# YOCO step on one Trainium2 core: layer 0's sample states decayed by ScalarE a stage earlier, value rows spread from two row groups, and layer 1's attention turn split off

## The reference, cut to what matters

```python
def gla_recurrent(q, k, v, g, s0):
    def step(s, xs):
        qt, kt, vt, gt = xs
        s = jnp.exp(gt)[..., None] * s + kt[..., None] * vt[..., None, :]
        return s, jnp.einsum('bhk,bhkv->bhv', qt, s)
```

```python
        p1 = jax.nn.softmax(jnp.einsum('bqhd,bkhd->bhqk', qf[..., :DH_B], k1) + bias, axis=-1)
        p2 = jax.nn.softmax(jnp.einsum('bqhd,bkhd->bhqk', qf[..., DH_B:], k2) + bias, axis=-1)
        return jnp.einsum('bhqk,bkhv->bqhv', p1 - lam * p2, vf)
```

## Time and profile before

| | before |
|---|---|
| median of 3 runs | 2008.17 us |
| profiled execution, whole | 2010.52 us |
| its span | 2008.7 us |
| TensorE matmul busy | 78% |
| VectorE busy | 38% |
| ScalarE busy | 19% |
| GpSimd busy | 17% |
| DMA, mean over the span | 280 GB/s |
| mean granted TensorE clock | 0.876 |

### The profile page before, as it was taken

How to read it: one execution, slowest core, us unless ns; L and a number is a source line. 1 busy time by engine, 2 the same in 40 slices (tenths; PEclk the granted TensorE clock), 3 DMA queues, 4 the chain that set the end, 5 groups by cost and what they waited for, 6 DMA issues and landing times. The chain is left out here.

```text
span 2008.7 us, 22067 instructions
## 1 busy us (share of the span) xinstructions
PE 1573.5 (78%) x7466; PEld 723.7 (36%) x7467; DVE 762.4 (38%) x1300; ACT 390.5 (19%) x755; POOL 341.1 (17%) x266
## 2 busy tenths in 40 slices
PE   6999976767479998936899887777587499989960
PEld 3333335233233333303356553344343233333320
DVE  1010125486300000136855567996385300000008
ACT  1010022022021221222120002334222012222212
POOL 0000000000000000022745566550000000000004
PEclk8989997589599999967999988889888699999985
DMA  8652620531699899979969999884422599999962
GB/s 329 254 218 84 253 85 1 186 135 53 262 406 427 337 383 430 390 285 347 355 241 393 402 375 404 338 321 164 145 92 94 217 372 377 422 428 427 429 258 93
DMA packets 122908, 563.02 MB, mean 280 GB/s; under 512 B 13621, under 2 KB 43126, under 8 KB 101307
## 3 DMA queue, kind: packets, MB, share of 16 engines
q1 hardware_dynamic: 98450, 496.63, 62.4%
q10 hardware_dynamic: 15424, 33.08, 4.3%
q0 software_dynamic: 8944, 32.15, 4.3%
HBM read 521.80 MB, written 40.03 MB: 280 GB/s over the span
## 5 line engine op out<-in xcount | busy, mean ns | idle before, releaser
L1483 PE MATMUL ps<-arena_w,arena_r 128*64 128x512 f32 x1664 | 379.2, 612 | 33.7 <-issue 28.8
L1483 PEld LDWEIGHTS ps<-arena_w,arena_r 128*64 128x64 f32 x1664 | 126.3, 142 | 280.4 <-issue 274.1
L1465 PE MATMUL ps<-arena_w,arena_r 128*64 128x512 f32 x832 | 190.1, 605 | 19.3 <-ACT arena_r L1513 19.3
L1560 DVE TENSOR_TENSOR arena_r<-arena_r,ps 128x512 f32<-128x512 f32 x38 | 26.1, 688 | 442.7 <-ACT arena_r L1530 442.7
L1863 POOL TENSOR_TENSOR arena_w<-arena_w,arena_r 128x1024 f32<-128x1024 f32 x48 | 114.9, 2400 | 110.3 <-DMA arena_w<-in_cache_k_dram 109.9
L1916 PE MATMUL ps<-arena_w,xt 128*128 128x256 f32 x512 | 123.8, 404 | 1.4 <-ACT xt L2081 1.4
L1863 POOL TENSOR_TENSOR arena_r<-arena_r 128x1024 f32<-128x1024 f32 x48 | 116.0, 2419 | 52.4 <-DMA arena_r<-in_cache_k_dram 52.1
L447 PE MATMUL ps<-arena_w,xt 128*128 128x512 f32 x256 | 112.5, 596 | 0.4 <-PE ps L206 0.4
L999 PE MATMUL ps<-arena_w,xt 128*128 128x512 f32 x256 | 111.4, 593 | 0.0
L1916 PEld LDWEIGHTS ps<-arena_w,xt 128*128 128x128 f32 x512 | 102.7, 203 | 17.9 <-ACT xt L2081 1.5
L1465 PEld LDWEIGHTS ps<-arena_w,arena_r 128*64 128x64 f32 x832 | 57.4, 139 | 125.7 <-issue 103.9
(11 more groups left out here) (367 smaller groups left out, 1978.8 us busy)
## 6 DMA issues: line engine op xcount, KB each, us to landing
arena_w<-in_w_exp_gate_dram SPq DMA_DIRECT2D x38, 2048.0 KB, 15.4
arena_w<-in_w_exp_up_dram SPq DMA_DIRECT2D x38, 2048.0 KB, 16.6
arena_w<-in_w_exp_down_dram SPq DMA_DIRECT2D x38, 2048.0 KB, 17.0
arena_m<-in_cache_v_dram SPq DMA_DIRECT2D x128, 512.0 KB, 7.9
arena_w<-in_cache_k_dram SPq DMA_DIRECT2D x64, 512.0 KB, 8.6
arena_r<-in_cache_k_dram SPq DMA_DIRECT2D x64, 512.0 KB, 9.8
arena_w<-in_w_ada_dram SPq DMA_DIRECT2D x12, 2048.0 KB, 16.8
arena_m<-in_w_ada_dram SPq DMA_DIRECT2D x12, 2048.0 KB, 8.7
```

The lines of the kernel that those rows point to most:

```text
L1465: last = nc.tensor.matmul(psy[c][at:at + 64, :], ht[u][:, k, 64 * (1 - a):64 * (2 - a)], wd[u][:, k, c * 512:(c + 1) * 512], start=(k == 0 ...
L1483: last = nc.tensor.matmul(ps[at:at + 64, :], xgt[u][:, k, 64 * a:64 * (a + 1)], w[u][:, k, :], start=(k == 0), stop=(k == KT - 1), tile_po ...
L1560: V.tensor_tensor(hs[u], es[u], psu[:, :], ALU.mult).then_inc(h_ok, 1)
```

## The change

Layer 0: the states are loaded into `arena_m`, at the head of SyncE's queue in the prompt's stage and ahead of the fill of `y_rows` (whose source becomes `m.x`). ScalarE decays them there, 32 activations between its own steps, and the sample stage starts at the products. The upper half of each value row is written a second time, to partitions 32 to 39; there are two selectors, at partitions 0 and 32, and the two spreading products sit in different row groups of the array. Layer 1: `turn(u - 2)` (the turning part of `finish`) is issued ahead of `scores(u)`; `keep` moves from VectorE to ScalarE; the two maxima become one instruction; ScalarE's `c_copy` comes ahead of `second_weight`; ScalarE issues the loads of the own value weights, after the wait it had anyway; the load at L1824 comes one step later.

```diff
@@ stage_gla_project, ScalarE
+                if c == 1:
+                    nc.scalar.copy(m.v[32:32 + NS, NTT - 1, 512:1024], m.ps[1][0:NS, :])
@@ stage_gla_prompt
+    m.st, src = view(m.M, 0, NS * HA, DVA), a["state_gla"].rearrange("l b h k v -> k (l b h) v")
+            def decay(b0, b1):
+                for b in range(b0, b1):
+                    s.wait_ge(st_in[b // 2], 16)
+                    for h in range(HA):
+                        nc.scalar.activation(m.st[:, b * HA + h, :], m.st[:, b * HA + h, :], ACT.Copy, scale=eg[:, h, b:b + 1])
+            nc.scalar.activation(eg, m.gs, ACT.Exp).then_inc(eg_ok, 1)
...
             exponents(2)
+            s.wait_ge(eg_ok, 1)
+            decay(0, 2)
             key_rows(2)
             output(1)
             exponents(3)
+            decay(2, 4)
             key_rows(3)
+            decay(4, 6)
             output(2)
+            decay(6, 8)
             output(3)
@@ stage_gla_prompt, SyncE
+            for n in range(NS // 2):
+                c = slice(2 * n * HA, 2 * (n + 1) * HA)
+                sp.dma_start(m.st[:, c, :], src[:, c, :]).then_inc(st_in[n], 16)
@@ stage_gla_sample, GpSimd
-            nc.gpsimd.memset(sel, 0.0).then_inc(sel_ok, 1)
+            for n in range(2):
+                nc.gpsimd.memset(sel[n], 0.0).then_inc(sel_ok, 1)
+            for n in range(2):
+                g.wait_ge(sel_ok, n + 1)
+                blocks = sel[n].rearrange("r (b n) -> r b n", n=P)
+                nc.gpsimd.affine_select(out=blocks, in_=blocks, compare_op=ALU.not_equal, fill=1.0, base=0,
+                                        pattern=[[-1, NS], [0, P]], channel_multiplier=1).then_inc(dg_ok, 1)
@@ stage_gla_sample, VectorE
-                v.wait_ge(st_in[b // 2], 16)
-                for h in range(HA):
-                    nc.vector.tensor_scalar(st[:, b * HA + h, :], st[:, b * HA + h, :], eg[:, h, b:b + 1], None, ALU.mult)
-                v.wait_ge(vb_mm, b + 1)
-                v.drain()
+                v.wait_ge(vb_mm, 2 * b + 2)
@@ stage_gla_sample, TensorE
-                    last = nc.tensor.matmul(m.ps[2 * (b % 2) + n][:, :], sel[:, b * P:(b + 1) * P],
-                                            m.v[0:NS, NTT - 1, n * 512:(n + 1) * 512], start=True, stop=True)
-                last.then_inc(vb_mm, 1)
+                    nc.tensor.matmul(m.ps[2 * (b % 2) + n][:, :], sel[n][:, b * P:(b + 1) * P],
+                                     m.v[32 * n:32 * n + NS, NTT - 1, n * 512:(n + 1) * 512], start=True, stop=True,
+                                     tile_position=(32 * n, 0)).then_inc(vb_mm, 1)
@@ stage_decoder, SyncE
-            for c in range(QCH):
-                sp.wait_ge(sp_mm, QCH + c + 1)
-                sp.dma_start(own_w[c], dec.source(a, 2 * QCH + c)).then_inc(mk_in[c], 16)
...
-                if g >= LAG and (g - LAG) % 4 == 1:
+                if g >= LAG and (g - LAG) % 4 == 2:
@@ stage_decoder, TensorE: finish(u) without its turning part, now turn(u)
                 for n, u in enumerate(dec.units(g)):
+                    if u >= dec.DEPTH:
+                        turn(u - dec.DEPTH)
                     scores(u)
@@ stage_decoder, ScalarE
             def own_rows(c):
                 s.wait_ge(sp_mm, c + 1)
                 nc.scalar.copy(shares[c % 2], OWN[c % 2][:, 0:CW]).then_inc(spa_cp, 1)
+                if c < 2 * QCH:
+                    s.dma_start(own_w[c - QCH], dec.source(a, c + QCH)).then_inc(mk_in[c - QCH], 16)
...
+            def keep(u):
+                h, i = u // NQ, u % NQ
+                s.wait_ge(o_mm, u + 1)
+                s.wait_ge(r_ok, u + 1)
+                nc.scalar.activation(m.v[:, i, h * DVB:(h + 1) * DVB], O_B[:, (u % 2) * DVB:(u % 2 + 1) * DVB], ACT.Copy,
+                                     scale=r1[i]).then_inc(o_ev, 1)
...
+                    if u >= dec.DEPTH:
+                        c_copy(u - dec.DEPTH)
+                    if u > dec.DEPTH:
+                        keep(u - dec.DEPTH - 1)
                     if u:
                         second_weight(u - 1)
-                    if u >= dec.DEPTH:
-                        c_copy(u - dec.DEPTH)
                     powers(u)
@@ stage_decoder, VectorE: keep gone; weigh waits for o_ev of unit u - 4 and gives r_ok
-                for j in range(2):
-                    last = V.tensor_reduce(out=mx[u % NB][:, j:j + 1], in_=SP[u % NB][j][:, 0:w], axis=AX.X, op=ALU.max, negate=True)
-                last.then_inc(nb_ok, 1)
+                V.tensor_reduce(out=mx[u % NB], in_=view(m.W, 1024 * (u % NB), 2, 512)[:, :, 0:w], axis=AX.X, op=ALU.max,
+                                negate=True).then_inc(nb_ok, 1)
```

More of the change, by code:

```diff
@@ L557, in stage_gla_prompt @@
     eend = [m.small[:, 480 + 4 * u:484 + 4 * u] for u in range(2)]
+    st_in = [sem(f"st_in{n}") for n in range(NS // 2)]
+    eg_ok = sem("eg_ok")
+    m.st, src = view(m.M, 0, NS * HA, DVA), a["state_gla"].rearrange("l b h k v -> k (l b h) v")
+    eg = take(HA, NS)
+    assert off[0] <= 9984
     kl_ps = [m.ps[u][:, :].rearrange("p (h k) -> p h k", k=P) for u in range(2)]
@@ L757, in stage_gla_sample @@
     sem = lambda n: ctx.enter_context(m_semaphore(nc, f"glas_{n}"))
[L758 to L761, removed]
+    sel_ok, dg_ok, vb_mm, s_ok, o_mm, o_out, qs_ok = (sem(n) for n in
+        ("sel_ok", "dg_ok", "vb_mm", "s_ok", "o_mm", "o_out", "qs_ok"))
+    st = m.st
     off = HA * TOK
-    eg = view(m.R, off, HA, NS)
     qsel = view(m.R, off + 32, HA, NS * NS)
-    sel = m.R[0:NS, off + 32 + HA * NS * NS:off + 32 + HA * NS * NS + NS * P]
-    src = a["state_gla"].rearrange("l b h k v -> k (l b h) v")
+    sel = [m.R[32 * n:32 * n + NS, off + 32 + HA * NS * NS:off + 32 + HA * NS * NS + NS * P] for n in range(2)]
     dst = a["s_sample"].rearrange("l b h k v -> k (l b h) v")
@@ L1758, in stage_decoder @@
     lm = [m.small[:, 52 + i:53 + i] for i in range(2)]
+    rinv = m.small[:, 54:55]
     col = m.small[:, 64:96].rearrange("p (v k) -> p v k", k=KT)
@@ L1986, in scores, with turn @@
                 last.then_inc(sc_mm, 1)
-            def finish(u):
-                h, i = u // NQ, u % NQ
+            def turn(u):
+                i = u % NQ
                 pe.wait_ge(dl_ok, u + 1)
@@ L1996, in finish @@
                 last.then_inc(c_tr, 1)
+            def finish(u):
+                h, i = u // NQ, u % NQ
                 pe.wait_ge(c_cp, u + 1)
@@ L2063, in _ @@
                         for late in range(u - dec.DEPTH + 1, u + 1):
+                            turn(late)
                             finish(late)
@@ L2188, in _ @@
                         second_weight(u)
+                        keep(u - dec.DEPTH)
                         for late in range(u - dec.DEPTH + 1, u + 1):
                             c_copy(late)
+                            keep(late)
                 v = g - LAG
@@ L2316, in attend @@
                     weigh(u - 1)
-                if u > dec.DEPTH:
-                    keep(u - dec.DEPTH - 1)
                 block_scores(u)
@@ L2321, in attend @@
                     weigh(u)
-                    for late in range(u - dec.DEPTH, u + 1):
-                        keep(late)
             v.wait_ge(pad_ok, 1)
@@ L2396, in _ @@
             v.drain()
+            v.wait_ge(o_ev, NQ * HB)
             V.memset(m.xt[:, :, TOK:SEQ + 32], 0.0)
```

33 lines of the change are left out of this document (10 added, 23 removed).

## The result

The changed kernel takes 2000.45 us (median of 8 runs, 1992.27 to 2006.85) against 2009.87 us for the kernel before beside it (8 runs, 2004.94 to 2013.24): ratio 0.9941, 95% interval 0.9924 to 0.9957. Run once more unedited in another group it took 1994.19 us against 2011.42: 0.9911 (0.9884 to 0.9937). By the medians the change is faster by 9 and 17 us, by the ratios (which are not quotients of the medians) by 12 and 18 us; 28.6 were forecast, and 2000.45 lies above the predicted range. The profiled execution of the changed kernel took 1992.27 us, the fastest of its eight, and that of before stood at its median: the 18.3 us between the two traces are more than the change is worth on average.

A forecast was written before the change was run, and what follows sets the result against it. TensorE at its low clock was taken to bound layer 0's samples' stage; memory, then VectorE, layer 1's attention until 1366 us, then alternating waits. Gains 10.6 + 5 + 1 + 5 + 7 = 28.6 us gave 1980 us, range 1963 to 1998.

The forecast's parts named there:

- Row groups: Layer 0's samples' stage: spread in two row groups takes 2.1 us instead of 3.71; gain 10.6 us, bounds -2.0 to some 21.
- Rivals a and e: Samples' stage: a, row groups do not overlap for 8 rows, 1993 us, chance 0.1; e, full clock, 1970 us, 0.1.
- Decays on ScalarE: Layer 0's prompt stage: eight decays cost at most 3.0 us and fit into existing waits; cost 0.
- Own value weights: Layer 1's projections: ScalarE issuing these loads removes TensorE's waits before the first value load; gain 5 us, bounds -2.8 to 7.2.
- Rival c: Layer 1's projections: own weights land no sooner whoever issues them, so 5 us are not won; 1985 us, chance 0.15.
- Load at L1824: Layer 1's memory-bound part: issuing this load one step later avoids SyncE's 8.9 us wait; gain 1 us, between 0 and 8.9.
- VectorE's part of a unit: Layer 1's units: moving `keep` and joining the maxima saves 0.25 to 0.35 us a unit; gain 5 us, between 0 and 7.7.
- Split turn: Layer 1's units after 1366 us: turn ahead of `scores` makes the copy early, covering `finish`'s wait; gain 7 us, bounds 0 and 11.7.
- rival d: Layer 1's units: the turn delays `scores` on the path, up to 44 us in 32 units; 2036 us, chance 0.05.

## Why the prediction was wrong, point by point

The direction was right, the size was not: two terms of the sum, 12 of 28.6 us, didn't come, both for want of a price on what the moved step puts in front of others.

- **Row groups, forecast 10.6: right.** 11.3 us in the stage, of which 10.6 belong to them by themselves. The estimate of 2.1 us for four records from the row of `scores` held (2.00), the clock stayed at 0.52, and GpSimd's second matrix cost 2.07 for my 2.02. Rivals a and e are out.
- **Decays on ScalarE, 0: right,** with the wrong bound (3.3 us for eight, not 3.0). What the decays' absence is worth to VectorE, which I left out, is 0.7 us.
- **Own value weights, forecast 5: wrong, about 0.** The first value load did not come sooner (B is 90.1 against 90.2). The failed step is "four issues on ScalarE's queue at 0.70 us". That row was from 977 us. The four loads of the earlier trace rows that lasted 12.70 us stood in the same row group, and I read their length as what SyncE suffered by its place, not as what any engine suffers that issues there. Rival c had the outcome, not the mechanism: the weights didn't stay late, ScalarE's own copies became late instead. The Trainium skill ("DMA: Bandwidth & Descriptors", Issuing engines are not separate DMA queues) says that initiating DMAs on several engines saves only the sequencer's time for it, "which is usually small relative to the DMA itself". The first half agrees with B; the second doesn't hold for two of the four issues of the kernel with the issue moved only: they took 6.90 and 9.18 us, and its four loads landed 18.7 to 25.2 us after their issue.
- **Load at L1824, forecast 1: open.** SyncE's wait of 8.9 us there is gone. C is 192.7 to 198.0 us with and without it, so a microsecond can't be seen.
- **VectorE's part of a unit, forecast 5: not refuted in size (7.0, interval 2.6 to 11.5, with the split turn behind `scores` in it), wrong in place as far as it can be seen.** I counted it only up to the last page, where it can't be told from D's scatter; 4.1 us came behind it, some 3 of them by `keep`, which I had priced at its own 0.25 us and not at its wait for TensorE's product. That its size came out is in part luck. One maximum for 128x1024 took 1.22 us where two took 1.28.
- **Split turn, forecast 7: wrong, and in E of the other sign.** VectorE's wait for `powers` did shrink (by 7.7 us). The failed step is "that copy is early and the wait of `finish` is covered by `scores`": TensorE still waited 11.8 us behind the last page where it had waited 11.7, because the copy and `keep` stand on ScalarE's queue behind `powers` of another unit, which waits for VectorE. And the step has a reverse that I put into rival d at 0.05: `scores` is now behind the turn, and VectorE waits 20 us for it. Rival d's price of 44 us was that of every unit; what counts is where TensorE, not VectorE, is late for the unit: behind a sample's row, behind a page's values, behind a wait for `keep`. That makes some 3.5 us of loss in E instead of 7 of gain. The comparison "at full width that is 2.2 + 1.1 us against some 3.5" looked at units that follow one another and left out what else stands on TensorE's queue between them, and the narrow units, whose `scores` can stand behind the turn of a full-width one.

With the measured terms the sum is 11.3 + 0 + 7.0 - 3.5 = about 15 us, between the 9 and 18 of the two timed groups. Layer 1's terms alone give 3.5 of it, where layer 1's part alone measured 6.3 us by the medians and at least 4.2 by the interval of its ratio. So the two terms account for most of the miss, and a few microseconds of layer 1 stand in no term.

## What to carry to other kernels

An issue of a DMA is an instruction with a length of its own: price it by issues of the same stretch, and expect whoever issues there to stand still that long; put it on an engine for which nobody waits, and spread it. A step moved ahead to be early for one engine is late for the engine that waited for the step it passed: list both waits, and price the second in the units where the moving engine is itself late. And an input that is ready sooner helps only if the engine that takes it up is free then: look what stands ahead of that step on its own queue. Where a stage has a strict beat, one timeline was enough to forecast it within 1 us.

## What the runs showed of the hardware

- **The length of an issue.** One `dma_start` of a weight block of 1 MB takes between 0.57 and 9.18 us on ScalarE within 27 us, in a stretch in which key pages and weights are in flight; four key loads on SyncE 16.40 us. What it waits for the profile doesn't say.
- **Two row groups, 8 rows each.** Four fp32 records of 512 columns at 1.2 GHz take 2.00 us in two row groups and 3.71 in one, 1.86 times less.
- **The clock after a shorter pause.** With TensorE idle for 2.38 us instead of 5.96 ahead of the samples' stage, its first eight records took 2.25 us at a granted clock of 0.85 instead of 3.78 at 0.50, so the upper level of 2.4 GHz for the larger part; from the next group on the clock was 0.50, the lower level, again:

```profile
360.11 2.25 PE L829 MATMUL ps<-arena_w 8*128 8x512 f32 x8 [2.38 <-DVE arena_r L808]
363.02 1.04 PE L838 MATMUL ps<-arena_m,arena_r 128*8 128x256 f32 x8 [0.67 <-DVE arena_m L812]
363.99 2.08 PE L829 MATMUL ps<-arena_w 8*128 8x512 f32 x4
```

- **GpSimd's select against VectorE.** Subtractions of two SBUF operands of 128x256 took 1.31 us beside the selects (1.17 and 1.25 us) and 0.42 otherwise; one of 128x512 beside GpSimd's memsets took 0.69 us, as elsewhere. The Trainium skill ("SBUF — State Buffer", SBUF: two separate sides) says that such a VectorE instruction and a GpSimd instruction that reads SBUF exclude each other for their whole length; the trace agrees.
